# The next weight slab's split ahead of the rotated tile, in the index keys' group of both mixers

## The reference

```python
def token_mix(h, cos, sin, w_in, sgu_w, sgu_b, w_out):
    p = h @ w_in
    ...
    q = partial_rope(p[..., OFF_Q:OFF_K].reshape(B, S, ATT_HEADS, ATT_HEAD_DIM), cos, sin)
    k = partial_rope(p[..., OFF_K:OFF_V].reshape(B, S, ATT_HEADS, ATT_HEAD_DIM), cos, sin)
    ...
    qi = partial_rope(p[..., OFF_IQ:OFF_IK].reshape(B, S, IDX_HEADS, IDX_HEAD_DIM), cos, sin)
    ki = partial_rope(p[..., OFF_IK:OFF_IW][:, :, None, :], cos, sin)[:, :, 0, :]
    wi = p[..., OFF_IW:PROJ_WIDTH]
    b_out = dsa_attention(q, k, v, qi, ki, wi)
```

## Time and profile before

| | |
|---|---|
| device time, median of 3 runs | 3000.38 us |
| the runs | 3000.38, 3000.57, 2998.42 us |
| profiled execution, its own time | 2999.97 us |
| its span, first to last instruction | 2998.2 us |
| mean granted TensorE clock | 0.993 |
| TensorE busy | 2948.5 us, 98% |
| VectorE busy | 2238.7 us, 75% |
| ScalarE busy | 1318.8 us, 44% |

### The profile page before, as it was taken

How to read it: one execution, slowest core, us unless ns; L and a number is a source line. 1 busy time by engine, 2 the same in 40 slices (tenths; PEclk the granted TensorE clock), 3 DMA queues, 4 the chain that set the end, 5 groups by cost and what they waited for, 6 DMA issues and landing times.

```text
span 2998.2 us, 47467 instructions
## 1 busy us (share of the span) xinstructions
PE 2948.5 (98%) x18016; PEld 2608.7 (87%) x18016; DVE 2238.7 (75%) x3253; ACT 1318.8 (44%) x1975; POOL 189.1 (6%) x267
## 2 busy tenths in 40 slices
PE   8999999999999999999999999999999999999998
PEld 7888888787999889998787899988998878799987
DVE  7577766655877788877688787778777678788753
ACT  4432323465555345442345555425454244654442
POOL 0000001200000000000130000000000023000000
PEclk9999999999999999999999999999999999999999
DMA  4366564411333633345332133462335432133332
GB/s 159 100 195 192 180 210 138 132 44 57 99 105 109 216 125 99 102 143 172 94 91 64 57 106 105 147 217 87 108 107 182 122 105 85 43 92 100 103 106 77
DMA packets 268334, 357.77 MB, mean 119 GB/s; under 512 B 19907, under 2 KB 211765, under 8 KB 268177
## 3 DMA queue, kind: packets, MB, share of 16 engines
q1 hardware_dynamic: 241344, 270.57, 28.8%
q0 software_dynamic: 26352, 84.74, 8.8%
q10 hardware_dynamic: 480, 0.29, 0.0%
HBM read 348.69 MB, written 2.10 MB: 117 GB/s over the span
## 4 chain that ended last, share of the span: by engine, by line
PE 85%; DVE 9%; ACT 2%; issue 2%; DMA 1%; POOL 0%; DVEq 0%; SPq 0%; ACTq 0%
PE bank L2313 16%; PE bank L2315 15%; PE bank L2314 15%; PE bank L2459 11%; PE bank L2461 11%; PE bank L2462 11%; DVE w_lo L1371 1%; ACT w_hi L780 1%; PE bank L2336 1%; PE bank L2337 1%; PE bank L2339 1%; DVE h_f L1427 1%; PE bank L2374 1%; DMA swap<-st 1%; DVE h_lo L1433 1%
## 5 line engine op out<-in xcount | busy, mean ns | idle before, releaser
L780 ACT ACTIVATE w_hi<-raw 128x1024 fp32r<-128x1024 f32 x308 | 325.8, 1058 | 749.0 <-PE bank L2315 706.0
L1371 DVE TENSOR_TENSOR w_lo<-raw,w_hi 128x1024 fp32r<-128x1024 f32 x288 | 351.9, 1222 | 369.0 <-ACT w_hi L780 366.2
L2313 PE MATMUL bank<-act_hi,w_hi 128*128 128x512 f32 (+1 forms) x1120 | 438.7, 392 | 0.0
L2315 PE MATMUL bank<-act_hi,w_lo 128*128 128x512 f32 (+1 forms) x1120 | 436.4, 390 | 0.0
L2314 PE MATMUL bank<-act_lo,w_hi 128*128 128x512 f32 (+1 forms) x1120 | 435.9, 389 | 0.0
L2313 PE MATMUL bank<-h_hi,w_hi 128*128 128x512 f32 x1056 | 417.5, 395 | 6.7 <-DVE w_lo L1371 6.1
L2314 PE MATMUL bank<-h_lo,w_hi 128*128 128x512 f32 x1056 | 412.7, 391 | 0.0
L2315 PE MATMUL bank<-h_hi,w_lo 128*128 128x512 f32 x1056 | 412.6, 391 | 0.0
L2459 PE MATMUL bank<-s_tile,w_hi_more 128*128 128x256 f32 x1200 | 339.8, 283 | 0.3
L2462 PE MATMUL bank<-s_tile,w_lo_more 128*128 128x256 f32 x1200 | 339.6, 283 | 0.0
L2461 PE MATMUL bank<-s_tile,w_hi_more 128*128 128x256 f32 x1200 | 339.6, 283 | 0.0
(11 more groups left out here) (383 smaller groups left out, 6282.7 us busy)
## 6 DMA issues: line engine op xcount, KB each, us to landing
raw<-in_ffn_w_in_dram SPq DMA_DIRECT2D x176, 512.0 KB, 3.5
ada_w<-in_ada_w_dram POOLq DMA_DIRECT2D x72, 1024.0 KB, 5.6
raw<-in_ffn_w_out_dram SPq DMA_DIRECT2D x88, 512.0 KB, 3.6
raw<-in_ffn_w_gate_dram SPq DMA_DIRECT2D x44, 512.0 KB, 3.8
raw<-in_ffn_w_up_dram SPq DMA_DIRECT2D x44, 512.0 KB, 3.8
raw<-in_ffn_w_down_dram SPq DMA_DIRECT2D x44, 512.0 KB, 4.1
raw<-in_mix_w_in_dram SPq DMA_DIRECT2D x44, 512.0 KB, 3.7
raw<-in_attn_w_qkv_dram SPq DMA_DIRECT2D x24, 512.0 KB, 3.6
```

The lines of the kernel that those rows point to most:

```text
L780: nc.scalar.activation(w_hi[:, nb % SPL, :], raw_slab(nb), ACT.Copy).then_inc(s_hi, 1)
L1371: V.tensor_tensor(w_lo[:, nb % SPL, :], raw_slab(nb), w_hi[:, nb % SPL, :].bitcast(F32), ALU.subtract).then_inc(s_lo, 1)
L2313: T.matmul(dst, wh, mh, start=first, stop=False)
L2315: return T.matmul(dst, wl, mh, start=False, stop=last)
```

## The change

On ScalarE and VectorE, in a group of one slab, the split of the slab two ahead (slab 4) is put first in the slot, ahead of what is left of the rotated tiles of the group before. In groups of two slabs the order stays. No instruction is added or removed.

```diff
@@ ScalarE, project
                     for j in range(slabs):
                         slot = 2 * g + j
+                        if slabs == 1:
+                            split_hi(n + 2)
                         if j == 0 and turned:
                             rotated_hi(*turned[0])
                         if m and slot in INDEX_SLOTS:
                             relus(4 * INDEX_SLOTS.index(slot))
                         if rotary and j == slabs - 1:
                             staged_tiles(g, tiles)
-                        if slot < 23:
+                        if slot < 23 and slabs == 2:
                             split_hi(n + 2 + j)
@@ VectorE, project
                         if m and slot in INDEX_SLOTS:
                             index_sums(4 * INDEX_SLOTS.index(slot))
+                        if slabs == 1:
+                            split_lo(n + 2)
                         if j == 0:
                             rotate(turned[0:1])
                             if slabs == 1:
...
                         if rotary and j == slabs - 1:
                             take_rotated(g, tiles, first)
-                        if slot < 23 if m == 0 else n + 2 + j - nb < POOL_LO[0]:
+                        if slabs == 2 and (slot < 23 if m == 0 else n + 2 + j - nb < POOL_LO[0]):
                             split_lo(n + 2 + j)
```

## The result

The changed kernel took 3001.66 us (median of 22 runs, 2998.06 to 3004.12); the kernel before, run beside it, 2997.99 us (22 runs, 2994.19 to 3001.94). The ratio is 1.0012, with a 95% interval of 1.0007 to 1.0018: +3.6 us, between 2.1 and 5.4. It is slower, by less than 0.2%. Forecast was +4.0 us. The runs of one kernel are spread over 6 to 8 us, so the difference shows in many runs only. The two profiled executions (2999.97 and 3001.95 us) differ by 2.0 us in their totals, and they are read here stretch by stretch: ahead of the first mixer's group, where both programs do the same, the changed one happened to be 2.58 us earlier already (end of slab 2 at 1471.66 instead of 1474.24).

A forecast was written before the change was run, and what follows sets the result against it. TensorE, busy 98% of a 2998.2 us span, was taken as the bound. Terms of -1.2 and +2.4 us plus two spells of 1.4 us gave +4.0 us, 3004.4 us against the median; range 2999.5 to 3007.5.

The forecast's parts named there:

- the rival of +1.2 us: In both mixers the clock stays up during the waits ahead of slab 5: only +1.2 us, 3001.6 us; chance 0.18.
- The wait ahead of slab 4 goes, and was not lost time: First mixer: TensorE's 2.39 us wait ahead of slab 4 vanishes, but without it TensorE would have stood before slab 5.
- The wait moves to slab 5, which hangs on the key tile's rotation: First mixer: wait grows to some 3.5 us ahead of slab 5; key tile's rotation follows the first query tile's by 6.87.
- First mixer -1.2, second +2.4 us at the start of slab 5: TensorE starts slab 5 1.2 us sooner in the first mixer and 2.4 us later in the second.
- Two spells of 1.4 us: Low clock in slab 5 of each mixer after its wait, 0 to 1.78 us possible, taken as 1.4 us each.
- The slower rival: Key tile's swap transfers meet slab 8's load and land after 3.5 us, both mixers: +8.3 us, 3008.7; chance 0.09.
- The gain without the price: Slab 5 comes in time in the first mixer, 4.5 us won; with the second's 0.66, -5.1 at most, 2995.3; chance 0.05.
- Range and sign: Whole kernel: 2999.5 to 3007.5 us; chance 0.89 within 0.2%, 0.09 slower by more, 0.02 faster by more.

The follow-up runs named there:

- the run with the first mixer alone: Changed kernel with the new order kept in the first mixer only, the old order in the second; 0.9999 of the kernel before, -0.3 us.
- the run with the second mixer alone: Changed kernel with the new order kept in the second mixer only, the old order in the first; 1.0011 of the kernel before, +3.3 us.
- the ScalarE run: Kernel before with only slab 4's high part moved first on ScalarE, its low part left in place on VectorE; 1.0009 of the kernel before, +2.7 us.

## Why the prediction was right

The time (+4.0 us forecast, +3.6 measured, interval 2.1 to 5.4) lies in the range, and the mechanism is the one forecast. The range itself is wide: it holds no change and the rival of +1.2 us as well, so the traces, not the time, tell these apart. That +4.0 came so near +3.6 is partly luck, as the runs leave 1.5 to 1.8 us to either side and the parts in the traces add up to 4.6.

- *The wait ahead of slab 4 goes, and was not lost time.* Both shown: the slabs follow one another at 5.44 us, and in the kernel before without its spell slab 5 starts no sooner.
- *The wait moves to slab 5, which hangs on the key tile's rotation.* Shown by the timeline, and by the runs in which slab 5's parts go ahead of that tile: the wait is gone. Forecast were 6.87 us from one rotation to the other; measured 6.85 and 6.86. What the chain adds up from rows of the kernel before could be relied on because every link of it stood in one of them. That the swap transfers decide there, by 0.1 to 0.2 us over VectorE's own path, fits the order of the rows, but was not tried by itself.
- *First mixer -1.2, second +2.4 us at the start of slab 5.* Measured -0.97 and +2.38. The first is off because the swap there landed 0.3 us later against slab 2 than in the profile before; it is a landing, and it moves from run to run (over the five profiles of kernels with slab 4 first on both engines in the first mixer, the rotation began 2.2 to 3.0 us after slab 2 had released ScalarE). In the run with the first mixer alone and in the one with TensorE kept busy ahead of slab 5, it starts in the first mixer 15.29 and 15.47 us after slab 2's last matmul; with the old order it is 15.86 to 16.17 in three profiles. So the gain there is between 0.4 and 1.3 us, depending on the execution.
- *Two spells of 1.4 us.* Two came, of 1.57 and 1.61 us by the timeline. The full price of 1.78 us taken from slab 4 of the kernel before was nearer than the 1.4 I took, and the reason given for taking less did not apply here: no part of a spell passed while TensorE waited, both began 0.4 to 0.5 us after slab 5 had (1487.02 against 1486.55, 2432.51 against 2432.10). It can happen: in the run with the second mixer alone, TensorE still waited for slab 4 of the first mixer when the clock fell (0.72 granted on average from 1478.60 to 1479.11, the start of slab 4), and that spell made slab 4 1.59 us longer instead of 1.78. Of the 0.2 us between 1.57 and 1.78, some 0.1 lies in what is compared: slab 5 of the kernel before starts with two matmuls 0.33 us apart (1490.10 and 1490.43), where later ones start 0.23 apart. The rest is left open. The rival in which the clock stays up (+1.2 us) is out for these executions, and the interval of the run with TensorE kept busy (-2.4 to +3.3) holds that time.
- *The slower rival*, the swap transfers meeting the load of slab 8, did not happen in the changed kernel: they landed after 1.7 to 1.8 us, the load having been issued some 3.5 us ahead. The mechanism is real, as the ScalarE run shows (3.4 us), but by these two cases it hangs on the moment: there the load went out within 0.1 us of the last transfer (2417.87 and 2417.8), while in the first mixer of the kernel before it went out 0.4 us after the last one (1482.42 and 1482.0), and all four landed after 1.7 to 1.8 us. The share of 0.08 that the prediction sets beside those covers only the time up to 1482.45.
- *The gain without the price* would have needed slab 5 in time. A further step that does this brings -4.5 us, near the -5.1 worked out for it, but only once the ReLU, too, is moved out of the way.
- *Range and sign.* "Within 0.2%" was right as the bound was put; the loss is resolved all the same, since 22 runs of each tell more apart than 6 us.

By an estimate from the figure of the Trainium skill (DMA: Bandwidth & Descriptors, "Anatomy of one DMA"), about 2.0 us fixed for a transfer, the sum would have been 0.5 us higher. 1.7 to 1.8 us were measured for the key tile's swap transfers before and after the change, and 3.0 to 3.5 us for four that were issued just after a load had gone out.

## What to carry to other kernels

A wait at the head of the list is worth only the distance to the next late part: before moving work forward, work out the start of the *next* slab from the chain behind the moved pair. On engines that keep their order, an instruction that must wait for the bottleneck belongs behind work that is ready already, unless that work can wait as well; here the same edit was even in one mixer, where the work it overtook was not ready either (its swap had not landed), and lost 3.3 us by the runs and 4.0 by the trace in the other. A moved wait can also change in kind: where the next slab is late anyway, the spell of low clock after the wait costs nothing; where it is not, the spell is paid for.

## What the runs showed of the hardware that was not expected

Waits of TensorE of nearly the same length may or may not be followed by the low clock. In the ScalarE run, waits of 2.03 us and of 1.67 us (first mixer, ahead of slabs 4 and 5) left the clock at 1.00 (first two rows), and one of 1.95 us in the second mixer brought a spell at half clock (third row; windows of TensorE):

```profile
1475.64:1479.10 3.46, 3.46 (x15) 1.00 0.57 163
1483.38:1486.80 3.42, 3.42 (x15) 1.00 0.66 182
```
```profile
2427.70:2431.10 3.40, 3.40 (x10) 0.50 0.61 179
```

All seven waits of 2.39 us and over ahead of slabs 4 and 5 in these profiles were followed by a spell. The Trainium skill (TensorE: Matmul & The Clock Gate, section on the HAM clock gate) has the number of slow matmuls vary from run to run of one kernel, at its start; these rows show the like among the waits of one execution. The length of a wait alone does not say whether the clock falls.
